# Four reorderings in a transformer block on one NeuronCore: value transposes, high halves, PSUM sums and a last tile in halves

## The reference

```python
proj = x @ w_in
branches = einsum('bsnc,ncd->bsnd', [y_a, y_b, y_c, y_d], w_branch)
merged = sum(sigmoid(g) * branches, axis=2)
h = layer_norm(ALPHA * x + merged @ w_out, ln1_g, ln1_b)
ffn = peer_ffn(h, peer_wq, peer_subkeys, peer_u, peer_v)
out = layer_norm(ALPHA * h + ffn, ln2_g, ln2_b)
# stick-breaking: a = exp(log_sigmoid(z) + reverse_cumsum(log_keep) - log_keep), log_keep = log_sigmoid(-z)
```

## Time and profile before

| | us |
|---|---|
| median of three runs | 1721.88 (1721.55 to 1725.12) |
| profiled execution | 1719.63 |
| its span | 1717.9 |
| PE busy | 1678.1 |
| DVE busy | 1239.9 |
| ACT busy | 775.3 |
| POOL busy | 820.3 |
| mean granted clock of PE | 0.993 |

### The profile page before, as it was taken

The page is one execution under the profiler, slowest core; times in us unless marked ns, Lnnn a source line. Parts: engine busy times, 40 slices in busy tenths (PEclk is TensorE's granted clock), DMA queues, the critical chain, the costliest instruction groups (busy, mean ns, idle before and its releaser), DMA issues.

```text
span 1717.9 us, 24437 instructions
## 1 busy us (share of the span) xinstructions
PE 1678.1 (98%) x8981; PEld 1481.6 (86%) x8981; DVE 1239.9 (72%) x2498; ACT 775.3 (45%) x1311; POOL 820.3 (48%) x496
## 2 busy tenths in 40 slices
PE   8999899999989999999999999999999999999997
PEld 6678677778879999999999999999888888888886
DVE  3487796552271976889887988435888888888886
ACT  4445545522223544774576377533333333333342
POOL 6232232344454566876866776785333323322312
PEclk9999999999999999999999999999999999999999
DMA  5111112224322465998899789998999999999952
GB/s 202 62 62 50 62 62 74 86 86 147 123 87 86 130 212 174 351 371 303 267 359 375 235 304 373 393 368 294 405 390 348 377 384 357 376 376 355 381 191 86
DMA packets 126359, 417.63 MB, mean 243 GB/s; under 512 B 12961, under 2 KB 32417, under 8 KB 124705
## 3 DMA queue, kind: packets, MB, share of 16 engines
q1 hardware_dynamic: 70176, 232.81, 38.9%
q0 software_dynamic: 36864, 134.23, 20.8%
q10 hardware_dynamic: 19200, 49.03, 7.3%
HBM read 364.91 MB, written 50.86 MB: 242 GB/s over the span
## 4 chain that ended last, share of the span: by engine, by line
PE 91%; DVE 5%; ACT 1%; issue 1%; DMA 1%; POOL 0%; ACTq 0%; SPq 0%; DVEq 0%; POOLq 0%
PE ps L1301 17%; PE ps L1302 17%; PE ps L1303 17%; PE ps L1529 11%; PE ps L1530 11%; PE ps L1532 11%; PE ps L1627 5%; PE ps L1365 1%; PE ps L1413 1%; PE ps L1396 1%; DMA raw<-w_units 0%; ACT w_hi L543 0%; DMA u_got<-u_rows,eid 0%; DVE x_tok L1016 0%; DVE dist_a L853 0%
## 5 line engine op out<-in xcount | busy, mean ns | idle before, releaser
L1301 PE MATMUL ps<-tok_hi,w_hi 128*128 128x384 f32 (+2 forms) x1544 | 549.0, 356 | 13.8 <-ACT gates L549 7.1
L543 ACT ACTIVATE w_hi<-raw 128x1024 fp32r<-128x1024 f32 x334 | 353.2, 1058 | 414.8 <-PE ps L1532 301.8
L1303 PE MATMUL ps<-tok_hi,w_lo 128*128 128x384 f32 (+2 forms) x1544 | 539.6, 350 | 0.0
L1302 PE MATMUL ps<-tok_lo,w_hi 128*128 128x384 f32 (+2 forms) x1544 | 539.6, 349 | 0.0
L490 POOL TENSOR_TENSOR w_lo<-raw,w_hi 128x1024 fp32r<-128x1024 f32 x128 | 318.5, 2491 | 164.3 <-ACT w_hi L543 163.9
L443 POOL TENSOR_TENSOR w_lo<-raw,w_hi 128x1024 fp32r<-128x1024 f32 x80 | 195.5, 2448 | 313.5 <-ACT w_hi L543 313.3
L1301 PEld LDWEIGHTS ps<-tok_hi,w_hi 128*128 128x128 f32 x1544 | 291.0, 188 | 46.1 <-issue 13.6
L1303 PEld LDWEIGHTS ps<-tok_hi,w_lo 128*128 128x128 f32 x1544 | 290.9, 188 | 18.7
L1302 PEld LDWEIGHTS ps<-tok_lo,w_hi 128*128 128x128 f32 x1544 | 291.2, 189 | 16.7
L1529 PE MATMUL ps<-w_hi,gh_hi 128*128 128x512 f32 x768 | 298.8, 389 | 0.0
L1530 PE MATMUL ps<-w_lo,gh_hi 128*128 128x512 f32 x768 | 298.8, 389 | 0.0
(11 more groups left out here) (216 smaller groups left out, 1848.8 us busy)
## 6 DMA issues: line engine op xcount, KB each, us to landing
raw<-u_units SPq DMA_DIRECT2D x128, 512.0 KB, 4.5
raw<-v_rows SPq DMA_DIRECT2D x128, 512.0 KB, 6.5
raw<-w_units SPq DMA_DIRECT2D x78, 512.0 KB, 3.4
gate_d<-stage ACTq DMA_DIRECT2D x12, 2048.0 KB, 12.0
gelu_d<-gelu_t ACTq DMA_DIRECT2D x120, 192.0 KB, 5.1
gelu_in<-gelu_d SPq DMA_DIRECT2D x30, 768.0 KB, 7.6
gate_in<-gate_d SPq DMA_DIRECT2D x28, 768.0 KB, 12.2
gate_in<-gate_d SPq DMA_DIRECT2D x2, 1536.0 KB, 17.8
```

What stands on the lines that cost most here:

```text
L543: act.activation(w_hi[:, n % RAW, :], raw[:, n % RAW, :], ACT.Copy).then_inc(hi_done, 1)
L1301: pe.matmul(out_, l_hi, r_hi, start=start, stop=False)
L1302: pe.matmul(out_, l_hi, r_lo, start=False, stop=False)
L1303: return pe.matmul(out_, l_lo, r_hi, start=False, stop=stop)
```

## The change

1. PE and ACT take the transposes of value unit 7 ahead of the last four index scores. In the filling, the transposes of a value unit come after the fourth chunk of the next unit instead of after its last, and ACT evicts them before that next unit's projection.
2. For D items, ACT's `keep_hi` moves behind the split and the eviction of the step (`keep_high`), and DVE's `keep_lo` behind the sums of the item before (`keep_low`).
3. In the merge two of four products and two of three sums are written into PSUM banks, each sum has one operand in PSUM, the high half is made by ACT instead of DVE, and the low half comes after two products of the next chunk. PE's waits are set anew: bank 3 of a chunk is now free when its low half is made.
4. In the first normalization the sum stays in PSUM, the factor g is taken there with the mean, and the root and b in one pass; POOL no longer takes part. The high and low halves of the first four wq units get their own 32 KB, so they need not wait for weight slots. The transposes of tiles 0 and 1 come earlier, within tiles 2 and 3.
5. The last tile of the second normalization: PE finishes column half 0, then half 1; DVE adds and takes statistics of a half as it comes, and the two halves are stored apart. ACT no longer scales it.

```diff
+    wq_hi = at("wq_hi", R + 36, [P, RAW, DM], F32R)
+    wq_lo = at("wq_lo", R + 52, [P, RAW, DM], F32R)
...
+    def merged(c):
+        return prod[1][:] if c == KC - 1 else branch_bank(c, 3)
...
             for n in range(4, U_EXP + LO_AHEAD):
-                if n in (U_WQ, U_WQ + 1):
-                    for t in ((0, 1) if n == U_WQ else (2,)):
-                        times_g(t, ln_g, norm1_set, scaled1_set)
-                if n == U_WQ + 5:
+                if n == U_WQ + RAW:
...
-                if n >= RAW:
+                if U_WQ <= n < U_WQ + RAW:
+                    act.wait_ge(prod_set, 4 * KC)
+                elif U_WQ + RAW <= n < U_EXP:
+                    act.wait_ge(unit_done, n - 2 * RAW + 1)
+                elif n >= RAW:
                     act.wait_ge(unit_done, n - RAW + 1)
...
+                if n == N_FIRST - 1:
+                    v_to_tokens(7)
                 if n >= N_IDX:
                     relu_scores(4 * (n - N_IDX))
-            v_to_tokens(7)
             v_to_tokens(8)
...
                 for n in units_in(s):
-                    unit(n)
+                    split_hi(n + HI_AHEAD)
                     if n - 1 in V_UNITS and n - 1 >= N_FIRST:
                         v_to_tokens(n - 1)
+                    projected(n)
+                if s + 1 < N_ITEM and kind_of(s + 1) == "D":
+                    keep_high(s + 1)
...
+            def merged_high(c):
+                act.wait_ge(merge_step, 3 * c + 3)
+                act.activation(m_hi[:, c, :], merged(c), ACT.Copy).then_inc(m_hi_set, 1)
...
+            for k in range(RAW):
+                split_hi(U_WQ + k)
             root(0, var_set, std_set)
...
                 if s >= 0:
                     weights(s)
+                if s + 1 < N_ITEM and kind_of(s + 1) == "D":
+                    keep_low(s + 1)
...
             for c in range(KC):
+                if c >= NH:
+                    merged_low(c - 1)
+                gated(c, 0)
+                gated(c, 1)
+                if 0 < c < NH:
+                    merged_low(c - 1)
+                dve.wait_ge(prod_set, 4 * c + 2)
+                dve.tensor_tensor(branch_bank(c, 3), branch_bank(c, 3), prod[2][:], ALU.add).then_inc(merge_step, 1)
+                gated(c, 2)
+                gated(c, 3)
                 dve.wait_ge(prod_set, 4 * c + 4)
+                dve.tensor_tensor(prod[1][:], branch_bank(c, 0), prod[1][:], ALU.add).then_inc(merge_step, 1)
+                dve.wait_ge(merge_step, 3 * c + 2)
+                dve.tensor_tensor(merged(c), branch_bank(c, 3), prod[1][:], ALU.add).then_inc(merge_step, 1)
+            merged_low(KC - 1)
...
+            def norm_first(t, meanwhile=lambda: None):
...
+                link(dve.scalar_tensor_tensor(z, x_tok[:, t, :], ALPHA, z, ALU.mult, ALU.add))
+                dve.bn_stats(stats[:, t, 0], ps[:, 2 * t, :])
+                link(dve.bn_stats(stats[:, t, 1], ps[:, 2 * t + 1, :]))
...
+                dve.scalar_tensor_tensor(z, z, mean_var[:, t, 0:1], ln_g[:], ALU.subtract, ALU.mult).then_inc(norm1_set, 1)
+                meanwhile()
...
+                dve.scalar_tensor_tensor(x_tok[:, t, :], z, rstd[:, one], ln_b[:], ALU.mult, ALU.add).then_inc(h_set, 1)
...
+            norm_first(2, lambda: (hT_low(0), hT_low(1)))
...
-                    pe.wait_ge(prod_set, 4 * (c - (2 if c < NH else 1)) + (2, 3, 1, 0).index(b) + 1)
+                    before = c - (2 if c < NH else 1)
+                    if b == 3:
+                        pe.wait_ge(m_set, before + 1)
+                    elif b == 0:
+                        pe.wait_ge(merge_step, 3 * before + 2)
+                    else:
+                        pe.wait_ge(prod_set, 4 * before + (1 if b == 2 else 3))
...
+                    if c == 3 and n - 1 in V_UNITS and n - 1 >= N_FIRST:
+                        v_to_tokens(n - 1)
                     if c == KC - 1:
                         last.then_inc(unit_done, 1)
-                        if n - 1 in V_UNITS and n - 1 >= N_FIRST:
-                            v_to_tokens(n - 1)
...
-                       lambda t, k: transpose_h(k - 1) if (t, k) in ((3, 1), (3, 2)) else None)
+                       lambda t, k: transpose_h(t - 2) if (t, k) in ((2, 2), (3, 0)) else None)
...
+            last_halves(U_END - RAW, NT - 1, lambda k: (gh_hi[:, k, :], gh_lo[:, k, :]), NT - 2)
```

More of the change, by code:

```diff
@@ L666, in _ @@
                         .then_inc(sig_kept, 1)
+            merged_high(KC - 1)
             for n in range(U_OUT, U_WQ - HI_AHEAD):
@@ L1533, in add_tile, with last_halves @@
                 return last
+            def last_halves(first, t, operands, column):
+                tile_ = slice(column * P, (column + 1) * P)
+                for a in range(2):
+                    o, cols = ps[:, 2 * t + a, :], slice(a * S, a * S + S)
+                    for k in range(RAW):
+                        s, (l_hi, l_lo) = (first + k) % RAW, operands(k)
+                        last = three(o, l_hi[:, tile_], l_lo[:, tile_], w_hi[:, s, cols], w_lo[:, s, cols],
+                                     False, k == RAW - 1)
+                    last.then_inc(last_full, 1)
             def last_units(first, tiles, ready, operands, full, between, before=0):
```

207 lines of the change are left out of this document (111 added, 96 removed).

## The result

The changed kernel took 1702.33 us (median of five runs, 1701.09 to 1705.58), against 1721.55 us before (1721.11 to 1725.12) in the same measurement: a ratio of 0.989, 95% interval 0.9879 to 0.9901, so 19.2 us or 1.1% faster. Its profiled execution took 1701.76 us (span 1700.0), 17.9 us less than the profiled one before. When the same kernel was run again later, one of its four executions took 2385 us with the clock at 0.66 on average; the ratios leave it out, the median printed with that run contains it.

A forecast was written before the change was run, and what follows sets the result against it. PE, busy 98% of the span, was taken as the bound, so only its waits, slowed clock and tail could shrink. Gains of 16.9 us took the profiled 1719.63 to 1702.7 us, the median to 1705.0; range 1696 to 1710.

The forecast's parts named there:

- The forecast case: Whole kernel: the gains of the five parts add to 16.9 us, giving 1705.0 us; chance 0.55.
- the places that were to show it: Named waits, clock levels and pass times, such as no PE wait before the first filling unit and merge sums at 0.69 us.
- the sum: Whole kernel: gains of 5.0, 1.3, 1.1, 3.6, 3.7 and 2.2 us, in all 16.9 us.
- the clock's share: Before the first filling unit: 6 us at clock 0.50 no longer follow the wait, a gain of 2.5 us.
- I keep the clock's fall after it: At unit 22: PE still waits some 4.2 us, and the clock still falls afterwards, so no clock gain is counted.
- The bound of part 2: Stick-breaking items: with no stall on any pass, waits of 6.3 and 0.4 and 2.6 of clock go, 9.3 us; otherwise -1.
- rival 1: At unit 22: the 6.3 us wait goes wholly, 8.2 us more gain, 1696.8 us; chance 0.22.
- Rival 2: Merge, before wq, item 11: new short waits bring the clock down, up to 1.7 us each, 1708.5 with two; chance 0.15.
- Rival 3: Stick-breaking items: port stalls accumulate to 17.6 us and reach the sliding-window items, about 1724 us; chance 0.02.
- Rival 4: Merge and first normalization: sums in PSUM still meet POOL, so both changes there give nothing, 1712 us; chance 0.04.

The follow-up runs named there:

- the third version: Changed kernel with POOL's splits held back, the merge's low half one product earlier, and DVE's low halves earlier in the first normalization: 1695.26 us.

## Why the prediction was right, and where not

1705.0 us was predicted and 1702.3 measured; on profiled executions 1702.7 against 1701.76. The forecast case came in, and the places that were to show it did. That the profiled times agree within 1 us is partly luck: the 1.5 us around `gelu_t` fell into that execution. Against the second profile of the changed kernel (1700.24 us) the gain is 19.4 us, as it is 19.2 by the medians, so 16.9 us was some 2.4 us short. By positions, parts 1 and 2 together gave 9.0 us up to the merge (7.4 forecast), part 3 3.9 (3.6), part 4 4.2 (3.7), part 5 1.7 (2.2), and 0.6 us between the first and the last matmul of `right` was no term of the sum.

- **Part 1** (6.3 us, and some 0.5 at unit 22 that the sum had under part 2). No wait before the first filling unit, clock 1.00 there. Of the two 0.8 us waits one left 0.23 us and one nothing. Undoing it cost 6.8 us at the first wq matmul and 4.9 to 5.5 in whole runs; some 1.7 us of the 6.8 (half of 6.8 less 3.4) are the longer fall at unit 22 there, which no term had. The waits were sized rightly; the clock's share, 2.5 us, was one of two values, since the same wait brought a fall of half the length in the run without part 1.
- **Part 2** (1.1 us). Its picture was right: one stall of 2.1 us in each of items 10 to 13 (2.2 forecast; in item 10 it took the softplus and not the multiplication, and items 14 and 15 had one too), a wait of 1.60 us before item 11's sums (1.4), one of 4.07 us at unit 22 (4.2), and a fall of the clock behind it. Two sizes were not. "I keep the clock's fall after it" took the fall of the kernel before, 6 us at 0.50; it was 3.5 us at 0.57, about 1.1 us cheaper. Which of the two lengths comes is chance as far as the runs show (last section). That is more than half of the 1.8 us by which PE's first wq matmul came earlier than the sum has it (12.6 forecast, 14.4 seen). And the gain wasn't part 2's. Without it, and with the earlier transposes of unit 20, the wait of 6.3 us was already down to 4.55 at unit 22 and 1.03 ahead of it; part 2 then traded waits of 6.0 us for 5.7, and by the medians gave nothing (1701.6 without it). The parts undone one by one add to 13.7 us (part 5 by its tails), against 19.2 for all. One reason is in the waits: each of parts 1 and 2 alone brings 6.3 us down to about 4.5 at unit 22, so the full wait stands only in the kernel before, where both are out. The rest of the gap isn't resolved, since each of these differences carries some 2 us of error.
- **The bound of part 2.** "With no stall on any pass", 9.3 us more, less 1.1, was rival 1's 8.2 us and 1696.8 us. Holding POOL back made nearly that case: 7.05 us up to the merge, 9.4 us by the medians (7.3 against the second profile of the changed kernel). The sum carried the right mechanism; that it could be had by one wait was not seen when it was written.
- **Part 3** (3.6 us, with a new wait of 1.6). The sums take 0.69 us, the new wait is 1.41 us and brings no fall. Undoing it cost 4.0 us. The 1.2 us wait, which the prediction puts ahead of the second late gate unit, stands ahead of the first, for chunk 2's first sum (to 344.97 us, PE goes on at 345.07); it went all the same. The numbers as printed add up to 3.5.
- **Part 4** (3.7 us, one wait of 1.2 left). One wait of 1.15 us was left; undoing it cost 3.8 us.
- **Part 5** (2.2 us). DVE ends 5.68 us behind PE's last matmul instead of 8.23: 2.5 us, as good as the 2.6 forecast. The stores took back 0.8 us and not 0.4: from DVE's end to the end of the span it is 3.9 us instead of 3.0, with three stores released within 0.7 us of one another. Net 1.7 us.
- **Rivals.** Rival 2 didn't happen: waits of 1.60, 1.41 and 1.15 us left the clock at 1.00. Rival 3 neither: there was a stall in nearly every stick-breaking item, but PE had no wait in the sliding-window items. Rival 4 is refuted by the merge's 0.69 us.

The rule weighed from the Trainium skill (SBUF — State Buffer, section "SBUF: two separate sides") was that a DVE pass with two SBUF inputs and a POOL operation that reads SBUF exclude each other. The trace agrees: `scalar_tensor_tensor` is held as the plain additions are the earlier trace rows (3.08 us for 0.96), POOL is held in turn when DVE was first (2.82 for 2.40), passes with a PSUM operand go on beside it (0.69 and 0.42 us), and nearly all of it goes with POOL's place (mean 975 and 425 ns).

## What to carry to other kernels

Before an engine's work is moved to fill a wait, look at what the move *releases*: ACT's earlier split brought POOL's forward onto DVE's passes, and the gain of the new order stayed hidden until POOL was made to wait for the last of these passes. Two causes of one wait can each be worth little alone; undoing or adding one part at a time then finds hardly an effect for either, and only the table of two by two shows them. And a step is late for the sake of every queue that it stands in: in the third version the wait stayed, because DVE's order was changed and ACT's was not read. Effects of 1 us drown in whole runs that scatter by up to 6 us; the positions of a few marker instructions in the profiles told them apart.

## What the runs showed that was not expected

- The length of a fall of the clock is not set by the wait ahead of it. 2.51 us of wait was followed by 0.50 and 0.60 in the two stretches of some 3.3 us behind it in one kernel, and by 0.55 and 0.94 in another. Six profiles have the same wait of 4.07 us at unit 22, in the same instructions: in four of them the clock stands at 0.50 for 3.4 us, in two for 6.8. The stretch from 180 to 185 us (PE, clock), first of the changed kernel's second profile, then of the second without part 5:

```profile
180.00:185.00 5.00, 5.00 (x32) 0.66 0.32 105
```

```profile
180.00:185.00 5.00, 5.00 (x24) 0.52 0.29 105
```

- Nor does its length alone say whether a fall comes. Waits of 1.60 us at item 11 and 1.41 us in the merge brought none. But the wait on a transfer near 34 us, 1.0 to 1.9 us long, was followed by a fall in the three profiles where it was longest (1.88, 1.81 and 1.75 us; 3.4 us at 0.50 each) and by none at 1.73 and 1.72 us. A term for the clock in a sum is therefore a choice between values, and whole runs of a kernel with such waits may scatter by it; only single executions were profiled, so how much is not shown. The Trainium skill (TensorE: Matmul & The Clock Gate, section "Part 1: The HAM clock gate (the "warmup" mystery)") says of the clock's rise at the start of work that its moment varies from run to run with where the first matmul lands. These rows show such a variation in the middle of a kernel.
- Small passes are held too. In the run with POOL held back, an addition of 128x2 elements took 1.98 us beside a later split, and 0.16 without one:

```profile
211.82 1.98 DVE L940 TENSOR_TENSOR small<-small 128x2 f32<-128x2 f32 x1
...
211.41 2.37 POOL L461 TENSOR_TENSOR w_lo<-raw,w_hi 128x1024 fp32r<-128x1024 f32 x1 [4.46 <-ACT w_hi L562]
```

These are in the sliding-window items, where PE has no wait; whether moving them would give anything wasn't tried.
